# Weights through two raw slots of 1 MB instead of four of 512 KB

## The chip, the cores and the metric

The kernel runs on one core of one Trainium2 chip. The metric is the device time of one execution in microseconds, here the median of several runs. The engines are TensorE (PE: matmuls, and weight loads into the array as PEld), VectorE (DVE), ScalarE (ACT), GpSimd (POOL) and SyncE (SP), which here does nothing but issue transfers. Each engine works through its own list in order, and waits on semaphores for the others.

## The reference

Four transformer layers follow one another on a sequence of 256 tokens with 1024 channels, all in f32. Each is a mixer and a hidden layer, with an RMS norm ahead of each:

```python
def first_block(x, ...):
    h = h + stick_breaking_attention(hn, w_sb_in[i], w_sb_out[i])      # layer 0, 16 heads
    h = h + squared_relu_mlp(rms_norm(h, g_mlp[0]), w_mlp_up[0], w_mlp_down[0])
    h = h + retention(hn, w_ret_in[i], w_ret_out[i])                    # layer 1, 4 heads
    h = h + squared_relu_mlp(rms_norm(h, g_mlp[1]), w_mlp_up[1], w_mlp_down[1])
    return rms_norm(h, g_final)
def second_block(x, ...):
    x = x + gla_mixer(hn, ...)                                          # gated linear attention
    x = x + conv_ffn(hn, ffn_w_up[0], ffn_conv_w[0], ffn_conv_b[0], ffn_w_down[0])
    x = x + nsa_mixer(hn, nsa_w_in[b], nsa_w_o[b], *nsa_shared_kv(x, ...))
    x = x + conv_ffn(hn, ffn_w_up[1], ...)
    return rmsnorm(x, norm_final)
```

All weight matrices together are 212 MB; each number of them is used once.

## The kernel before, in words

The host lays the weight matrices out as 212 pieces `ws[g]` of 128 partitions by 2048 f32 (`PIECE`), 1 MB each, in the order in which PE uses them. Pieces 0 to 15 belong to the stick-breaking attention (`G_SB`), then come MLP 0 (16 to 47), retention (48 to 79), MLP 1 (80 to 111), gated linear attention (GLA, 112 to 127), the first convolutional hidden layer (FFN, 128 to 160), the sparse attention (NSA, 161 to 178) and the second FFN (179 to 211).

A piece passes four engines:

- SP brings it to the raw ring `ring`, which has `RAW` = 4 slots of half a piece (`HALF` = 1024 columns, 512 KB). Half q = 2g or 2g+1 of piece g goes to slot q % 4. The function is `stream`; from the fifth half on it waits until DVE has read the slot's last content (`lo_ready`). Landing is told on `weights_in[q % 4]`.
- ACT rounds the half to fp32r, `w_hi` (`hi_half`, line 1228; the split below).
- DVE writes what the rounding left out, `w_lo` (`lo_half`, line 1701; the remainder below).
- PE multiplies in three matmuls of fp32r (`mm3`, lines 565 to 567): high by high, high by low and low by high. It waits per half piece on `lo_ready` (`split`) and tells on `done` that it has finished a piece.

`w_hi` and `w_lo` have `RING` = 4 slots of a whole piece. ACT's and DVE's function `refill(g)` waits (ACT on `done`) until PE has finished piece g, and then splits piece g + 4 into its slot, both halves in a row. The calls of `refill` stand in ACT's and DVE's lists at places that are written out by hand between their other work (norms, evacuations, softmax parts). Both engines work in order: whatever stands behind a split that waits for its transfer waits too.

At the start SP issues the four quarter pieces of x (`x_half`) between the first halves. In the stick-breaking attention ACT's list has the splits of pieces 5, 6 and 7, then the first pair's two sigmoids (`sb_sigmoids(0)`, lines 1364 and 1365), the splits of pieces 8 and 9, the second pair's sigmoids, and the copy of the first pair's transposed weights (`sb_copy(0)`, line 1369). PE's list has the transposes `sb_turn(0)` (line 772) ahead of piece 6, and the products `sb_av(0)` (line 783) in the middle of it; the first wait for the sigmoids (over DVE's scan, line 1918, and its product, line 1923, and POOL, line 420), the second for the copy. At the start of NSA, ACT's list has `refill(G_NSA + 2)`, `ns_raw_(0)` (lines 1534 and 1535), `refill(G_NSA + 3)`, `ns_raw_(1)`, the normed input (`tiles("7b", 0, ...)`), and so on, up to the gates (line 1611), which PE transposes.

Of the kernel before, what the change touches and what calls it, by code (L numbers as in the profile page):

```python
# [28 lines left out]
HALF = PIECE // 2  # L29
RAW = 4  # L30
# [43 lines left out]
G_END = 212  # L74
# [3 lines left out]
def build(nc, ws, small, narrow, tables, decay, rows, x_in, out):  # L78
    from contextlib import ExitStack
    ctx = ExitStack()  # L80
    with ctx:
        def sb(name, shape, dt=F32):
            return ctx.enter_context(nc.sbuf_tensor(name, shape, dt))

        def sem(name):
            return ctx.enter_context(nc.semaphore(name))

        ring = sb("ring", [P, RAW, HALF])
# [108 lines left out]
        x_loaded = [[sem(f"x_loaded{t}{c}") for c in range(2)] for t in range(TT)]  # L197
        quarter_done = sem("quarter_of_stage_done")
        tab_in, row_in = sem("tables_loaded"), sem("row_loaded")
        weights_in = [sem(f"weights_in{s}") for s in range(RAW)]  # L200
        hi_ready, lo_ready = sem("piece_hi"), sem("piece_lo")
        done = sem("piece_done")
        n_ready = sem("narrow_split")
# [20 lines left out]
        def plus(n, turn, each):  # L224

            return n if turn is None else turn * each + n
# [136 lines left out]
        @block.sync  # L363
        def _(sp):
            def x_half(t, c):
                v = slice(c * 512, (c + 1) * 512)
                sp.dma_start(h[:, t, v], x_in[t * P:(t + 1) * P, v]).then_inc(x_loaded[t][c], 16)

            def stream(q, turn=None):

                if turn is not None or q >= RAW:
                    sp.wait_ge(lo_ready, plus(q - RAW + 1, turn, RAW))
                g, c = q // 2, (q % 2) * HALF
                src = ws[g][:, c:c + HALF] if turn is None else \
                    ws[bass.ds(turn * (RAW // 2) + g, 1), :, c:c + HALF].rearrange("a p n -> p (a n)")
                sp.dma_start(ring[:, q % RAW, :], src).then_inc(weights_in[q % RAW], 16)

            x_half(0, 0)
            stream(0)
            stream(1)  # L380
            x_half(1, 0)
            x_half(0, 1)
            stream(2)
            x_half(1, 1)
            stream(3)
            turns = (2 * G_END - RAW) // RAW
            with sp.Fori(0, turns) as turn:
                for q in range(RAW, 2 * RAW):
                    stream(q, turn)
            for q in range(RAW + turns * RAW, 2 * G_END):  # L390
                stream(q)
            for t in range(TT):
                for c in range(2):
                    v = slice(c * 512, (c + 1) * 512)
                    sp.wait_ge(xs_ready[c], t + 1)
                    sp.dma_start(out[t * P:(t + 1) * P, v], xs[:, t, v]).then_inc(stored, 16)
            sp.wait_ge(stored, 32 * TT)
# [812 lines left out]
        def _(act):  # L1210
# [13 lines left out]

            def hi_half(q):
                c = (q % 2) * HALF
                act.wait_ge(weights_in[q % RAW], 16 * (q // RAW + 1))
                A(w_hi[:, q // 2 % RING, c:c + HALF], ring[:, q % RAW, :], ACT.Copy).then_inc(hi_ready, 1)  # L1228

            def hi(g):  # L1230
                hi_half(2 * g)
                hi_half(2 * g + 1)
# [101 lines left out]
            act.wait_ge(gains_ready, 1)  # L1334
            tiles(0, 0, part=(0, 1))
            hi_half(0)
            hi_half(1)
            tiles(0, 1, part=(0, 1))
# [345 lines left out]
        def _(dve):  # L1684
# [551 lines left out]
            def ns_cmp_p(c):  # L2236

                s, _, l = ns_cmp(c)
                dve.wait_ge(nsa_cmp_exp, c + 1)
                sees = tab[:, C_CMUL:C_CMUL + TT * CMP].rearrange("p (t n) -> p t n", n=CMP)[:, :, 0:1]  # L2240
                link(V.tensor_reduce(l, s, AX.X, ALU.add))
                link(V.reciprocal(l, l))
                link(V.tensor_tensor(l, l, ns_gate[:, :, 8 * c:8 * c + 8], ALU.mult))
                link(V.tensor_tensor(l, l, sees.broadcast_to([P, TT, 8]), ALU.mult))
                V.tensor_tensor(s, s, l.unsqueeze(3).broadcast_to([P, TT, 8, CMP]), ALU.mult).then_inc(nsa_cmp_p, 1)
# [327 lines left out]
```

## Time and profile before

| | |
|---|---|
| median of 3 runs | 1360.02 us (1358.62 to 1360.3) |
| the profiled execution's own time | 1360.86 us |
| its span, first to last instruction | 1359.1 us |
| PE busy | 1337.8 us, 98% |
| DVE, ACT, POOL busy | 907.8, 726.0, 121.3 us |
| `ring<-ws` transfers | 424 of 512 KB, median 4.8 us from issue to landing |
| read from HBM over the span | 169 GB/s |

The busy time of an engine is the union of its instructions. The profile's times start at the first instruction. "Landing" is the time from the issue of a transfer by SP to its last semaphore update. Idle time stands with what ended it.

### The profile page before, as it was taken

To read this page: it belongs to the slowest core of one execution; us is meant where nothing else is said; L and a number is where in the kernel's file an instruction comes from. 1 tells how busy PE (TensorE), PEld (TensorE's weight loads), DVE (VectorE), ACT (ScalarE), POOL (GpSimd) and SP (SyncE) were. 2 spreads that over 40 slices of the span, in tenths; PEclk is the share of its full clock that TensorE was granted. 3 is DMA by queue.
4 is the path that set the end of the run, shared out by engine and by line. 5 is a ranking of instruction groups with operands and counts; after the bars stand their busy time and mean duration, and the time that the engine had idled before them with its cause. 6 is when DMAs were issued, how large, how long until landed. Compare 5 with 4: busy or idle time off the path is not lost.

```text
span 1359.1 us, 23120 instructions
## 1 busy us (share of the span) xinstructions
PE 1337.8 (98%) x8826; PEld 1198.2 (88%) x8826; DVE 907.8 (67%) x1417; ACT 726.0 (53%) x1155; POOL 121.3 (9%) x123
## 2 busy tenths in 40 slices
PE   9999999999999999999999999999999999999998
PEld 8888989889987889999888889999988877999996
DVE  5757655557645647555567569777868775787776
ACT  6655544445334536444464457555557656665553
POOL 0002000002500000000001300000002233000000
PEclk9999999999999999999999999999999999999999
DMA  7535655555553456555554345555554411365551
GB/s 255 187 125 205 219 185 187 187 185 183 189 186 124 156 171 217 185 187 187 187 169 146 105 156 196 195 184 190 170 188 162 166 53 51 126 210 187 184 184 72
DMA packets 63887, 231.09 MB, mean 170 GB/s; under 512 B 7088, under 2 KB 7344, under 8 KB 63792
## 3 DMA queue, kind: packets, MB, share of 16 engines
q1 hardware_dynamic: 62208, 224.42, 49.2%
q10 hardware_dynamic: 1584, 5.31, 1.1%
q8 instruction: 70, 1.15, 0.3%
q14 instruction: 25, 0.20, 0.0%
HBM read 228.66 MB, written 1.05 MB: 169 GB/s over the span
## 4 chain that ended last, share of the span: by engine, by line
PE 89%; DVE 5%; ACT 2%; issue 2%; DMA 1%; POOL 1%; POOLq 0%; DVEq 0%; SPq 0%; ACTq 0%
PE ps L565 27%; PE ps L567 27%; PE ps L566 27%; DVE w_lo L1701 2%; PE ps L934 1%; DVE x_lo L1721 1%; ACT w_hi L1228 1%; PE ps L537 1%; PE ps L1094 1%; PE ps L1125 1%; DMA ring<-ws 1%; PE ps L1107 1%; ACT x_hi L1248 1%; PE ps L858 1%; PE ps L783 0%
## 5 line engine op out<-in xcount | busy, mean ns | idle before, releaser
L1701 DVE TENSOR_TENSOR w_lo<-ring,w_hi 128x1024 fp32r<-128x1024 f32 x424 | 514.8, 1253 | 174.2 <-ACT w_hi L1228 173.8
L1228 ACT ACTIVATE w_hi<-ring 128x1024 fp32r<-128x1024 f32 x424 | 429.5, 1052 | 232.8 <-PE ps L567 181.3
L565 PE MATMUL ps<-x_hi,w_hi 128*128 128x256 f32 x1600 | 455.0, 284 | 0.5 <-DVE x_lo L1721 0.5
L566 PE MATMUL ps<-x_lo,w_hi 128*128 128x256 f32 x1600 | 452.7, 283 | 0.0
L567 PE MATMUL ps<-x_hi,w_lo 128*128 128x256 f32 x1600 | 452.7, 283 | 0.0
L565 PEld LDWEIGHTS ps<-x_hi,w_hi 128*128 128x128 f32 x1600 | 306.8, 192 | 4.1 <-issue 3.0
L566 PEld LDWEIGHTS ps<-x_lo,w_hi 128*128 128x128 f32 x1600 | 306.9, 192 | 1.1
L567 PEld LDWEIGHTS ps<-x_hi,w_lo 128*128 128x128 f32 x1600 | 306.8, 192 | 0.0
L565 PE MATMUL ps<-w_hi,y_hi 128*128 128x512 f32 x560 | 220.3, 393 | 0.4 <-DVE y_lo L1753 0.4
L566 PE MATMUL ps<-w_lo,y_hi 128*128 128x512 f32 x560 | 218.3, 390 | 0.0
L567 PE MATMUL ps<-w_hi,y_lo 128*128 128x512 f32 x560 | 218.1, 389 | 0.0
L567 PEld LDWEIGHTS ps<-w_hi,y_lo 128*128 128x128 f32 x560 | 105.1, 188 | 22.3
L565 PEld LDWEIGHTS ps<-w_hi,y_hi 128*128 128x128 f32 x560 | 105.3, 188 | 21.9 <-issue 0.8
L565 PE MATMUL ps<-w_hi,x_hi 128*128 128x512 f32 (+1 forms) x304 | 122.7, 404 | 0.8 <-DVE w_lo L1701 0.8
L566 PEld LDWEIGHTS ps<-w_lo,y_hi 128*128 128x128 f32 x560 | 105.3, 188 | 20.1
L567 PE MATMUL ps<-w_hi,x_lo 128*128 128x512 f32 (+1 forms) x304 | 116.3, 383 | 0.0
L566 PE MATMUL ps<-w_lo,x_hi 128*128 128x512 f32 (+1 forms) x304 | 115.8, 381 | 0.0
L411 POOL TENSOR_TENSOR stat<-stat,power 128x1 f32<-128x1 f32 x20 | 11.7, 588 | 876.6 <-DVE stat L1696 695.5
L1748 DVE SCALAR_TENSOR_TENSOR arena<-ps,arena 128x512 f32<-128x512 f32 x64 | 44.0, 688 | 65.7 <-PE ps L567 63.9
L1314 ACT ACTIVATE arena<-arena,sm 128x256 f32<-128x256 f32 x88 | 48.2, 595 | 52.0 <-DVE arena L1748 52.0
L565 PEld LDWEIGHTS ps<-w_hi,x_hi 128*128 128x128 f32 x304 | 58.0, 191 | 15.9 <-issue 5.4
L1248 ACT ACTIVATE x_hi<-ps,sm 128x128 fp32r<-128x128 f32 x128 | 35.7, 377 | 63.9 <-PE ps L537 63.9
(219 smaller groups left out, 1260.8 us busy)
## 6 DMA issues: line engine op xcount, KB each, us to landing
ring<-ws SPq DMA_DIRECT2D x424, 512.0 KB, 4.8
tab<-tables ACTq DMA_DIRECT2D x3, 550.0 KB, 5.3
rowg<-rows ACTq DMA_DIRECT2D x3, 512.0 KB, 6.2
h<-x SPq DMA_DIRECT2D x4, 256.0 KB, 6.1
out<-arena SPq DMA_DIRECT2D x4, 256.0 KB, 2.2
arena<-decay ACTq DMA_DIRECT2D x1, 768.0 KB, 8.6
sm<-small ACTq DMA_DIRECT2D x1, 642.0 KB, 4.7
arena<-narrow ACTq DMA_DIRECT2D x1, 296.0 KB, 2.9
```

Source lines behind the costliest of these rows:

```text
L537: r = nc.tensor.transpose(ps[:, base + k // 2, t * T + (k % 2) * P:t * T + (k % 2 + 1) * P], h[:, t, k * P:(k + 1) * P], ident)
L565: mm(o, lh, rh, start=start, stop=False, skip_group_check=True)
L566: mm(o, lh, rl, start=False, stop=False, skip_group_check=True)
L567: return mm(o, ll, rh, start=False, stop=stop, skip_group_check=True)
L858: r = mm(ps[:, rt_o[hd][t], :], rt_s[:, hd, t * P:(t + 1) * P], rt_v[:, 0, hd * 512:(hd + 1) * 512], start=True, stop=t == 0)
L934: r = mm(o, keys, q, start=True, stop=True, skip_group_check=True)
L1094: r = mm(ps[:, 4 + i, P * t:P * (2 * t + 1)], ns_qr[v, pr, t * P:(t + 1) * P], ns_kd[v, br, pr // 2, 0:P * (t + 1)], start=t == 0, stop=Tr ...
L1228: A(w_hi[:, q // 2 % RING, c:c + HALF], ring[:, q % RAW, :], ACT.Copy).then_inc(hi_ready, 1)
L1248: r = A(dst[:, k, t * P:(t + 1) * P], ps[:, base + b, t * T + (k % 2) * P:t * T + (k % 2 + 1) * P], ACT.Copy, scale=gain(n, k))
L1314: r = A(conv[:, u % 2, e, :], conv_in[:, u % 2, e, :], ACT.Identity, scale=par(u, 4 + e), bias=par(u, 6 + e))
L1701: V.tensor_tensor(w_lo[:, g % RING, v], ring[:, q % RAW, :], w_hi[:, g % RING, v].bitcast(F32), ALU.subtract).then_inc(lo_ready, 1)
L1748: return V.scalar_tensor_tensor(dst, src.rearrange("p (a t) -> p a t", t=T), by, sc.unsqueeze(1).broadcast_to([P, 2, T]), ALU.mult, ALU.mult)
```

## The change

SP brings a piece in one transfer of 1 MB to a raw slot of a whole piece, of which there are two: slot g % 2 is the halves 2(g % 2) and 2(g % 2) + 1 of the same `ring`. The slot is free when both remainders of piece g - 2 are written. There are two landing semaphores instead of four, and both halves of a piece wait on the same one. At the start SP issues x's first quarter, piece 0, x's other three quarters, piece 1. What ACT, DVE and PE do, and their order, stays; each half is still split by itself.

```diff
-        weights_in = [sem(f"weights_in{s}") for s in range(RAW)]
+        weights_in = [sem(f"weights_in{s}") for s in range(RAW // 2)]
...
-            def stream(q, turn=None):
-
-                if turn is not None or q >= RAW:
-                    sp.wait_ge(lo_ready, plus(q - RAW + 1, turn, RAW))
-                g, c = q // 2, (q % 2) * HALF
-                src = ws[g][:, c:c + HALF] if turn is None else \
-                    ws[bass.ds(turn * (RAW // 2) + g, 1), :, c:c + HALF].rearrange("a p n -> p (a n)")
-                sp.dma_start(ring[:, q % RAW, :], src).then_inc(weights_in[q % RAW], 16)
+            def stream(g, turn=None):
+
+                if turn is not None or g >= 2:
+                    sp.wait_ge(lo_ready, plus(2 * g - 2, turn, RAW))
+                src = ws[g] if turn is None else ws[bass.ds(turn * 2 + g, 1), :, :].rearrange("a p n -> p (a n)")
+                dst = ring[:, 2 * (g % 2):2 * (g % 2) + 2, :].rearrange("p a n -> p (a n)")
+                sp.dma_start(dst, src).then_inc(weights_in[g % 2], 16)
 
             x_half(0, 0)
             stream(0)
-            stream(1)
             x_half(1, 0)
             x_half(0, 1)
-            stream(2)
             x_half(1, 1)
-            stream(3)
-            turns = (2 * G_END - RAW) // RAW
+            stream(1)
+            turns = (G_END - 2) // 2
             with sp.Fori(0, turns) as turn:
-                for q in range(RAW, 2 * RAW):
-                    stream(q, turn)
-            for q in range(RAW + turns * RAW, 2 * G_END):
-                stream(q)
+                for g in range(2, 4):
+                    stream(g, turn)
+            for g in range(2 + turns * 2, G_END):
+                stream(g)
...
-                act.wait_ge(weights_in[q % RAW], 16 * (q // RAW + 1))
+                act.wait_ge(weights_in[q // 2 % 2], 16 * (q // RAW + 1))
```

SP's list at the start of the program, with - for before and + for the change (`ring<-ws` is a piece or a half piece of the weights, `h<-x` a quarter of x):

```order
 L367 DMA h<-x 128x512
-L376 DMA ring<-ws 128x1024 x2
-L367 DMA h<-x 128x512 x2
-L376 DMA ring<-ws 128x1024
-L367 DMA h<-x 128x512
-L376 DMA ring<-ws 128x1024
...
+L375 DMA ring<-ws 128x2048
+L367 DMA h<-x 128x512 x3
+L375 DMA ring<-ws 128x2048
```

The four half-piece issues in front of the loop have become two issues of a whole piece, and the last three quarters of x now all stand between them.

ACT's list in the stick-breaking attention before, from the splits of piece 5 to the first split of piece 9 (`piece_done` is PE's `done`):

```order
L1228 ACTIVATE w_hi<-ring 128x1024 [waits weights_in2,piece_done]
L1228 ACTIVATE w_hi<-ring 128x1024 [waits weights_in3]
L1228 ACTIVATE w_hi<-ring 128x1024 [waits weights_in0,piece_done]
L1228 ACTIVATE w_hi<-ring 128x1024 [waits weights_in1]
L1228 ACTIVATE w_hi<-ring 128x1024 [waits weights_in2,piece_done]
L1228 ACTIVATE w_hi<-ring 128x1024 [waits weights_in3]
L1364 ACT_TABLE_LOAD
L1364 ACTIVATE arena<-ps 128x768 [waits sb_z]
L1365 ACTIVATE arena<-ps 128x768
L1228 ACTIVATE w_hi<-ring 128x1024 [waits weights_in0,piece_done]
L1228 ACTIVATE w_hi<-ring 128x1024 [waits weights_in1]
L1228 ACTIVATE w_hi<-ring 128x1024 [waits weights_in2,piece_done]
```

The same place of ACT's list in the change:

```order
L1225 ACTIVATE w_hi<-ring 128x1024 [waits weights_in1,piece_done]
L1225 ACTIVATE w_hi<-ring 128x1024 [waits weights_in1]
L1225 ACTIVATE w_hi<-ring 128x1024 [waits weights_in0,piece_done]
L1225 ACTIVATE w_hi<-ring 128x1024 [waits weights_in0]
L1225 ACTIVATE w_hi<-ring 128x1024 [waits weights_in1,piece_done]
L1225 ACTIVATE w_hi<-ring 128x1024 [waits weights_in1]
L1361 ACT_TABLE_LOAD
L1361 ACTIVATE arena<-ps 128x768 [waits sb_z]
L1362 ACTIVATE arena<-ps 128x768
L1225 ACTIVATE w_hi<-ring 128x1024 [waits weights_in0,piece_done]
L1225 ACTIVATE w_hi<-ring 128x1024 [waits weights_in0]
L1225 ACTIVATE w_hi<-ring 128x1024 [waits weights_in1,piece_done]
```

Nothing has moved; the first split of a piece now waits for the semaphore that its second half also waits for. Line numbers behind SP's part are three lower in the change.

## Rows read from the trace of the kernel before

**Rows 1.** The page: span, and busy us, share, instructions of each engine.

```profile
span 1359.1 us, 23120 instructions
...
PE 1337.8 (98%) x8826; PEld 1198.2 (88%) x8826; DVE 907.8 (67%) x1417; ACT 726.0 (53%) x1155; POOL 121.3 (9%) x123
```

**Rows 2.** PE's waits: waiting line, its releaser, us in total, times, longest.

```profile
PE ps L1160 <- ACT arena L1611: 2.3, 1, 2.3
PE ps L1107 <- POOL arena L507: 1.5, 1, 1.5
...
PE ps L537 <- DVE h L1775: 0.9, 1, 0.9
```

**Rows 3.** ACT's waits, whole span: its waits for a weight transfer.

```profile
ACT w_hi L1228 <- DMA ring<-ws: 50.7, 59, 3.6
```

**Rows 4.** Line 376 between 1118 and 1127 us: two halves, issued 7.4 us apart.

```profile
DMA to landing us min/median/max: 3.5/3.6/3.7
```

**Rows 5.** Line 376 between 237.5 and 239.5 us: two halves, with nothing else under way.

```profile
L376 SPq DMA_DIRECT2D ring<-ws x2: 332/332/333, 237.8 to 238.9; - x2
...
DMA to landing us min/median/max: 3.8/4.3/4.8
```

**Rows 6.** Line 376 between 1 and 2 us: the first two halves.

```profile
L376 SPq DMA_DIRECT2D ring<-ws x2: 424/424/425, 1.3 to 1.7; - x2
...
DMA to landing us min/median/max: 4.9/5.4/5.8
```

**Rows 7.** ACT's timeline, first 55 us: start, us, instruction, [idle before].

```profile
6.43 2.16 ACT L1228 ACTIVATE w_hi<-ring 128x1024 fp32r<-128x1024 f32 x2
...
31.33 2.00 ACT L1228 ACTIVATE w_hi<-ring 128x1024 fp32r<-128x1024 f32 x2
...
48.57 0.79 ACT L1364 ACTIVATE arena<-ps 128x768 f32<-128x768 f32 x1
...
49.95 0.81 ACT L1369 ACTIVATE arena<-ps 128x768 f32<-128x768 f32 x1
```

**Rows 8.** The chain of waits, 26 to 58 us: start, us, what.

```profile
34.94 5.75 DMA ring<-ws
40.71 1.06 ACT w_hi L1228
...
51.43 0.81 PE ps L783 x12
```

**Rows 9.** PE's timeline at 47.7 us.

```profile
47.69 0.87 PE L772 MATMUL ps<-sm,arena 128*128 128x128 f32 x6 [0.39 <-POOL arena L420]
```

**Rows 10.** SP's timeline at 19.3 us.

```profile
19.26 0.33 SPq L376 DMA_DIRECT2D ring<-ws  x1
```

**Rows 11.** The chain of waits, 984 to 994 us.

```profile
984.82 5.94 DMA ring<-ws
```

**Rows 12.** SP's timeline at 1006.7 us.

```profile
1006.74 0.33 SPq L376 DMA_DIRECT2D ring<-ws  x1
```

**Rows 13.** ACT's timeline at 1019.5 us.

```profile
1019.52 1.06 ACT L1228 ACTIVATE w_hi<-ring 128x1024 fp32r<-128x1024 f32 x1 [1.10 <-DMA ring<-ws]
```

**Rows 14.** DVE's timeline at 1037.2 us.

```profile
1037.24 3.32 DVE L1701 TENSOR_TENSOR w_lo<-ring,w_hi 128x1024 fp32r<-128x1024 f32 x2 [0.28 <-ACT w_hi L1228]
```

**Rows 15.** SP's timeline at 1064.4 us.

```profile
1064.44 0.33 SPq L376 DMA_DIRECT2D ring<-ws  x1
```

**Rows 16.** ACT's timeline, 1064 to 1080 us.

```profile
1068.64 2.08 ACT L1228 ACTIVATE w_hi<-ring 128x1024 fp32r<-128x1024 f32 x2
...
1073.20 0.43 ACT L1546 ACTIVATE arena<-ps 128x120 f32<-128x120 f32 x2 [0.22 <-PE ps L1039]
```

**Rows 17.** Two stretches: PE, PEld, DVE, ACT, POOL busy, granted clock, DMA share, GB/s.

```profile
1050.20:1052.20 2.00, 0.00 (x0) 0.00 (x0) 2.00 (x4) 1.48 (x3) 0.00 (x0) 1.00 0.20 68
1052.20:1059.00 6.80, 6.00 (x28) 5.22 (x29) 4.85 (x14) 5.40 (x13) 0.00 (x0) 0.50 0.82 270
```

**Rows 18.** ACT's timeline at 1275.1 us, in the second FFN.

```profile
1275.13 1.09 ACT L1314 ACTIVATE arena<-arena,sm 128x256 f32<-128x256 f32 x2 [2.28 <-DVE arena L1748]
```

## The prediction

> **What bounds the kernel now.** I read the page first: TensorE (PE) works in 1337.8 of 1359.1 us [rows 1]. So nothing on another engine costs time unless it makes PE wait, and every wait that it does make PE take is added to the end, since PE runs its list in order. The view of PE's waits shows few: the longest, 2.3 us, is for ScalarE (ACT) at line 1611 in the last attention [rows 2]. The weights' own row says where the change can bite: ACT stood 59 times, 50.7 us in all, waiting for a half piece to land [rows 3]. Nearly all of that is hidden now, because the four split slots `w_hi`/`w_lo` let PE run behind. It is not hidden where ACT's list holds something that PE needs soon behind a weight split.
>
> **What one transfer costs, L.** A half piece alone lands 3.5 to 3.7 us after its issue [rows 4]. Two halves issued 1.1 us apart land after 3.8 and 4.8 us [rows 5]: 5.9 us from the first issue for the whole megabyte. The trace has no 1 MB transfer. Lower bound: at the start, where the queue is full, halves issued at 1.3 and 1.7 us land after 4.9 and 5.8 us, at 6.2 and 7.5, so the second 512 KB takes 1.3 us more [rows 6]; 3.6 + 1.3 = 4.9 us. Upper bound: the pair's 5.9 us, as the same bytes pass the same engines. I take L = 5.3, an estimate between the two, because the second half of a pair starts 1.1 us late, when the engines are still at work on the first. The Trainium skill ("DMA: Bandwidth & Descriptors", "Anatomy of one DMA") gives 2.0 us plus the bytes by 436 GB/s, which makes 4.4 us; it fits transfers from another queue, and by it the sum below would be about 2 us. The half alone took 0.4 us more than that formula's 3.2 us here.
>
> **What the change does to a slot.** Before, a half slot is refilled once its own half is split; now both halves must be split, so a piece's transfer starts when only its second half used to start. The second half then lands about when it did (4.8 against L), the first about 1.1 + 5.3 - 3.8 = 2.6 us later, and the second split, which ran at the landing of its half, now runs 0.95 us behind the first (below). The 424 half issues become 212; SP only waits, so this saves nothing on the path. From the first split of a piece to the issue that its slot frees: the first split of piece 5 begins at 31.33 and the half that its slot lets through is issued at 34.94, 3.61 us [rows 7, 8]; two splits in a row take 2.00 us, each 1.06, so the second begins 0.95 behind the first. One slot thus turns round in L + 3.61 = 8.9 us for every second piece, where PE takes one piece each 6.4 us (1359.1 by 212 pieces): supply is enough, only its lateness counts.
>
> **Start.** The first piece lands at 7.5 instead of 6.2; the queue is full, so at the same time as its second half did. Its first split ran at 6.43 [rows 7], so PE starts 1.07 us late.
>
> **Term A, the first attention.** ACT has the splits of pieces 5, 6 and 7 in front of the first two sigmoids, and of 8 and 9 in front of the next two. Already now the chain passes through the second half of piece 7: issue 34.94, landing after 5.75, split 40.71, and then sigmoid, scan, product, and the transposes at 47.69, before which PE stood 0.39 us [rows 8, 9]. The odd pieces share a slot. The second half of piece 3 was issued at 19.26 [rows 10]; with the start's 1.07, piece 3 is now issued at 20.33, lands at 20.33 + L, and each next odd piece L + 3.61 later. Piece 7 lands at 27.55 + 3L = 43.5; its second split starts at 44.4 instead of 40.71, 3.7 us late, and PE stands about 3.0 us in front of the transposes (3.7 + 0.39 - 1.07). Piece 9 lands at 31.16 + 4L = 52.4; its two splits take 1.9 us to the start of the next operation [rows 7], so the second sigmoids start at 54.3 instead of 48.57, 5.7 us late. The copy after them (49.95, 0.81 us long) is what PE needs at 51.43: 0.67 us of cover [rows 7, 8]. **A = 4L - 16.2 = 5.0 us**, which contains the start and the first stall. The even pieces share the other slot and land between the odd ones, ahead of ACT. From piece 10 on ACT waits for PE to free a split slot before it splits, and the transfer is there by then.
>
> **Term B, the end of the first FFN.** The chain runs through the second half of piece 162, issued at 984.82, 5.94 us to landing, split at 990.79; PE then waits 0.9 us for the residual [rows 2, 11]. Now both halves come at 984.82 + L and the second split 0.95 later: **B = L - 5.02 = 0.3 us**.
>
> **Term C, the start of the last attention.** Piece 165 is issued at 1006.74 [rows 12], its slot is refilled 3.61 after it lands, so piece 167 lands at 1010.35 + 2L and its second split starts at 1011.30 + 2L = 1021.9 instead of 1019.52 [rows 13]. Behind it ACT has no pause until it has split the normed input, and VectorE (DVE) then runs without a pause but for 0.28 us at 1037.24 [rows 14] up to the gates for which PE stands 2.3 us: **C = 2L - 8.22 - 0.28 = 2.1 us**.
>
> **Term D, a little later.** Piece 175 is issued at 1064.44 [rows 15]; its second split starts at 1065.39 + L = 1070.7. Before, the two took 2.08 us from 1068.64, that is to say the second started at 1069.66. ACT is 1.0 us late and has 0.22 us of pause before the copy at 1073.20 [rows 16], from which the chain goes over DVE and GpSimd to PE's 1.5 us wait [rows 2]: **D = L - 4.5 = 0.8 us**.
>
> **Clock.** Before, PE had nothing to do from 1050.2 to 1052.2, and then its granted clock was 0.50 for 6.8 us, the 1.2 GHz level [rows 17]. The stall of 3.0 us that A makes near 48 us is longer. If it is answered in the same way, 6.8 us at half clock lose 3.4 us of matmuls, of which 5.0 - 3.7 = 1.3 us fall into time in which PE would stand anyway: between 0 and 2.1 us, and I take 1.2. The fall that exists at 1052 stays as it is.
>
> **What I cost at nothing.** In both FFNs one split in three arrives at a half that has just landed; its second split is now about 1.1 us later. It is hidden by ACT's own pause behind it (next work at 1275.13 after 2.28 us idle, waiting for DVE [rows 18]). If that pause were gone, each of some 14 such places would cost up to 1.1 us. The MLPs, retention and GLA splits run 5 us or more ahead of PE and wait for PE at the loop's pace; their first pieces come 1 to 2.5 us later and eat cover alone.
>
> **Sum.** 5.0 + 0.3 + 2.1 + 0.8 + 1.2 = 9.4 us. The profiled execution took 1360.86, so 1370.3; it lies 0.84 above the median of the three runs shown (1360.02), so **1369.4 us** as a median. With L = 4.9 and no fall of the clock: 3.4 + 0 + 1.3 + 0.4 = 5.1, so 1365. With L = 5.9: 7.4 + 0.9 + 3.3 + 1.4 + 2.1 = 15.1, so 1375.
>
> **Rivals.** (1) A megabyte lands fast. Its rows are 8 KB instead of 4 KB and half as many descriptors are written; at L = 4.4, half a microsecond under my lower bound, the terms are 1.4 + 0 + 0.3 + 0 = 1.7 us: 1361.7, no difference that shows. For it: the 1.3 us for 512 KB in a full queue [rows 6]. Against it: no pair in the trace comes near it. The Trainium skill's rule on that page ("Rules for kernel authors": at least 1 MiB per DMA for bandwidth) points this way; its page "Perfetto Trace Analysis", "DMA Optimizations", points the other way (smaller pieces may start sooner where the DMA engines are mostly idle); with this trace's chain waiting on the landing of a half at 40.7 us, the second agrees with it, and no run yet shows the first. (2) Faster: both chains of A and B run through halves that took 5.75 and 5.94 us because another half was in flight. One transfer per piece ends these collisions. But for a gain over 2.7 us the stalls behind them must vanish (0.4 + 0.9 + about 1.3 of the 2.3 us), and that needs L at 3.6, the time of half the bytes: about 1357. (3) The lateness adds up in the FFNs, where ACT is never far ahead: 14 times 0.6 us, 8 us on top, 1377. Against it: DVE there waits for PE in each chunk, so nothing accumulates. (4) ACT's order is more elastic than I think, and only the start's 1.07 and C remain: 3.2 us, 1363.
>
> **How the numbers follow.** Forecast with its mechanism (A to D, L from 4.9 to 5.9): 0.68. Rival 1: 0.14. Rival 2: 0.04. Rival 3: 0.07. Rival 4: 0.07. 0.2% of 1360 is 2.7 us, about what a measurement of this kernel can tell from nothing. Slower by more: 0.68 + 0.07 + most of rival 4, 0.80. Within: rival 1 and a part of rival 4, 0.16. Faster: 0.04. The range goes from 1362.5, where rival 4 begins, to 1375.5, where L = 5.9 ends; below it stand most of rivals 1 and 2 (0.15), above it 0.05 or so.
>
> **What the profile will show.** The median landing of `ring<-ws` at 5.3 us (over 5.9 or under 4.6 makes me wrong in size). PE's waits: a new one of about 3 us at the first attention's transposes (line 769 there, three up from 772), another of about 1.4 us at the products after them, the wait for the gates at 4.4 instead of 2.3, and the one on GpSimd at 2.3 instead of 1.5. ACT's waits for `ring<-ws` fewer, as the second half never waits, and longer. PE's granted clock at a half for some microseconds near 50. The time of the FFNs unchanged: the span from piece 140 to 158 to 0.2 us. I am wrong if PE's waits in the first 60 us stay under 2 us, or if the loss stands in the FFNs.

## The result, and the profile after

The changed kernel takes 1366.37 us, the median of five runs (1365.28 to 1368.22), against 1360.02 us before: 6.35 us more. The ratio to the runs of before is 1.005, its 95% interval 1.0038 to 1.0062, so it is slower by more than the 0.2% that a measurement can tell. The forecast was 1369.4 in a range from 1362.5 to 1375.5. The profiled execution took 1368.22, the slowest of the five, 7.36 us over the profiled one of before; a second profile of the same kernel (below) ended 4.54 us after before's, so what repeats has to be kept apart from what one execution shows. The lines of the changed part and behind stand three lower than before (L375 for L376, L1225 for L1228, L780 for L783).

The page and the queue of the weights, first that of after:

```profile
span 1366.5 us, 22278 instructions
...
PE 1339.5 (98%) x8826; PEld 1198.7 (88%) x8826; DVE 907.2 (66%) x1417; ACT 724.5 (53%) x1155; POOL 122.8 (9%) x123
...
q1 hardware_dynamic: 31680, 224.41, 45.6%
```

Against [rows 1], PE's busy time grew by 1.7 us of the 7.4; the rest is time in which it stood. The transfers' own engines are busy for less, not for more: 45.6% of the span against 49.2% for the same queue (`q1`) before.

What one transfer costs (the view of the tile `ring`), and ACT's waits for it (releaser, us in total, times, longest):

```profile
DMA to landing us min/median/max: 4.6/4.8/8.1
```

```profile
ACT w_hi L1225 <- PE ps L564: 167.8, 57, 7.5
ACT w_hi L1225 <- DMA ring<-ws: 110.5, 67, 4.5
```

The megabyte lands in 4.8 us, where I had taken 5.3. ACT's waits for it went from 50.7 us in 59 waits [rows 3] to 110.5 us in 67: longer, as I said, but not fewer. Sixty more us of waiting on ACT cost 6 us at the end: PE's waits, which follow, show that nearly all of them stand in front of a split that PE does not need yet.

PE's waits of after (waiting line, releaser, us in total, times, longest), to be read against [rows 2]:

```profile
PE ps L780 <- ACT arena L1366: 2.9, 3, 1.1
PE ps L1157 <- ACT arena L1608: 2.3, 1, 2.3
PE ps L769 <- POOL arena L417: 1.6, 1, 1.6
PE ps L1104 <- POOL arena L504: 1.6, 1, 1.6
PE ps L562 <- DVE y_lo L1718: 1.3, 1, 1.3
...
PE ps L534 <- DVE h L1772: 1.0, 1, 1.0
```

The transposes' wait at L769 grew from 0.39 [rows 9] to 1.6. The products at L780 waited once, 0.8 us near 85 us, before; that wait is unchanged and two of about 1 us are new. For `y_lo` PE waited once, 0.4 us, before; it now waits three times, the longest 1.27 us. The waits for the gates and for GpSimd, on which two of my terms ran, stand as they were. Where the waits lie is told by PE's timeline:

```profile
49.42 0.44 PE L769 MATMUL ps<-sm,arena 128*128 128x128 f32 x2 [1.61 <-POOL arena L417]
...
54.13 0.33 PE L780 MATMUL ps<-arena 128*64 128x128 f32 x2 [0.97 <-ACT arena L1366]
...
117.09 0.44 PE L780 MATMUL ps<-arena 128*64 128x128 f32 x4 [1.10 <-ACT arena L1366]
...
1036.78 1.99 PE L534 MATMUL ps<-sm,h 128*128 128x128 f32 x8 [0.40 <-DVE y_lo L1718]
...
1042.90 0.35 PE L562 MATMUL ps<-y_hi,w_hi 128*128 128x256 f32 x1 [1.27 <-DVE y_lo L1718]
```

The same two instructions of the first attention began at 47.69 and 51.43 before [rows 8, 9]: 1.73 and 2.70 us later now.

ACT's timeline shows what is late (each pair of splits is one piece; 5, 6, 7, 8 and 9 in this order):

```profile
33.11 2.01 ACT L1225 ACTIVATE w_hi<-ring 128x1024 fp32r<-128x1024 f32 x2 [1.20 <-DMA ring<-ws]
36.58 2.01 ACT L1225 ACTIVATE w_hi<-ring 128x1024 fp32r<-128x1024 f32 x2 [1.47 <-DMA ring<-ws]
41.50 2.01 ACT L1225 ACTIVATE w_hi<-ring 128x1024 fp32r<-128x1024 f32 x2 [2.90 <-DMA ring<-ws]
...
46.22 2.00 ACT L1225 ACTIVATE w_hi<-ring 128x1024 fp32r<-128x1024 f32 x2
49.97 2.01 ACT L1225 ACTIVATE w_hi<-ring 128x1024 fp32r<-128x1024 f32 x2 [1.75 <-DMA ring<-ws]
51.89 0.79 ACT L1361 ACTIVATE arena<-ps 128x768 f32<-128x768 f32 x1
...
53.27 0.81 ACT L1366 ACTIVATE arena<-ps 128x768 f32<-128x768 f32 x1
```

Pieces 5, 7 and 9 share a slot. Their first splits begin at 33.11, 41.50 and 49.97, a step of 8.4 us, which is 4.7 to 4.8 of landing and 3.65 to 3.72 from the landing to the next issue. The second sigmoids follow at 51.89 instead of 48.57, and the copy that PE needs at 53.27 instead of 49.95: 3.32 us late, of which 0.67 were covered [rows 7, 8], so 2.65, close to the 2.70 of PE's row.

A table of the lateness gives the whole sum: the time at which PE signals the end of a piece, less the same in the trace of before. The second line is the second profile of the same kernel (run e8_after_again).

| us later than before, at the end of piece | 0 (at 15 us) | 6 (55) | 14 (118) | 158 (986) | 160 (1000) | 165 (1030) | 167 (1044) | 169 (1060) | 176 (1151) | span |
|---|---|---|---|---|---|---|---|---|---|---|
| after | 0.48 | 2.77 | 3.94 | 3.94 | 4.02 | 4.01 | 7.01 | 7.13 | 7.39 | 7.4 |
| after, again | 0.20 | 2.56 | 4.54 | 4.49 | 4.41 | 4.40 | 5.20 | 4.20 | 4.56 | 4.6 |

The second line has 2.0 us between pieces 6 and 14, 1.2 of it at piece 14 as in the first; the other 0.8 goes with a wait of 0.7 us at the products at 63 us, behind piece 10, which landed in 7.4 us there and in 4.8 in the first profile.

From piece 14 to piece 158, 870 us with the MLPs, the retention, the GLA and a whole FFN, nothing is lost, and nothing behind piece 176. The same stretch, shifted by the 3.94 us (PE, PEld, DVE, ACT, POOL busy, granted clock, DMA share, GB/s), first before, then after:

```profile
130.00:980.00 850.00, 847.54 (x5334) 764.08 (x5333) 544.06 (x725) 429.31 (x596) 61.76 (x53) 1.00 0.53 178
```

```profile
133.94:983.94 850.00, 847.53 (x5334) 764.08 (x5333) 544.60 (x725) 429.10 (x596) 59.05 (x53) 1.00 0.50 178
```

### The profile page after: what moved, and what is told of

Its sections match the earlier page's. It is cut to its first block, busy times and chain, and to the rows that moved or that the text cites. A ratio compares the mean times of both kernels' runs of the same rounds, so it can differ in the third digit from the quotient of the medians.

```text
span 1366.5 us, 22278 instructions
## 1 busy us (share of the span) xinstructions
PE 1339.5 (98%) x8826; PEld 1198.7 (88%) x8826; DVE 907.2 (66%) x1417; ACT 724.5 (53%) x1155; POOL 122.8 (9%) x123
## 3 DMA queue, kind: packets, MB, share of 16 engines
q1 hardware_dynamic: 31680, 224.41, 45.6%
## 4 chain that ended last, share of the span: by engine, by line
PE 83%; DVE 7%; ACT 4%; DMA 4%; issue 2%; POOL 0%; SPq 0%; POOLq 0%; DVEq 0%; ACTq 0%
PE ps L562 25%; PE ps L564 25%; PE ps L563 25%; DMA ring<-ws 4%; DVE w_lo L1698 3%; ACT w_hi L1225 2%; PE ps L931 1%; DVE x_lo L1718 1%; PE ps L1122 1%; PE ps L1091 1%; PE ps L534 1%; ACT x_hi L1245 1%; PE ps L855 1%; PE ps L780 0%; DVE arena L2254 0%
## 5 line engine op out<-in xcount | busy, mean ns | idle before, releaser
L1225 ACT ACTIVATE w_hi<-ring 128x1024 fp32r<-128x1024 f32 x424 | 425.4, 1052 | 278.6 <-PE ps L564 167.8
L562 PEld LDWEIGHTS ps<-w_hi,x_hi 128*128 128x128 f32 x304 | 58.1, 191 | 16.2 <-issue 5.4
L564 PEld LDWEIGHTS ps<-w_hi,x_lo 128*128 128x128 f32 x304 | 58.0, 191 | 11.3
```

Source lines behind the costliest of these rows:

```text
L562: mm(o, lh, rh, start=start, stop=False, skip_group_check=True)
L564: return mm(o, ll, rh, start=False, stop=stop, skip_group_check=True)
```

## The experiments

Each was timed beside the kernel before, whose median was 1360.2 us with each of them. Unless it says otherwise, a time is the median of five runs.

### One half of the change at a time

The change has two effects on a piece: its transfer is issued only when both halves of the slot are free, and its first split runs only when all of it is there. The kernel before can have each with its 512 KB transfers. First the late issue alone:

```diff
-                    sp.wait_ge(lo_ready, plus(q - RAW + 1, turn, RAW))
+                    sp.wait_ge(lo_ready, plus(q - RAW + 2 - q % 2, turn, RAW))
```

> The kernel before with one part of the change: the first half of a piece is issued only when both remainders of the piece two before are written, right ahead of the second half; two transfers, four semaphores, each half still split as soon as it has landed. Theory M (what costs is when the halves can be split: a late issue and a landing that is told for both at once, read by ACT in order): here the first half lands some 3.7 us after the issue, the second about 4.9, so the second split is where it was before; 0 to 1.5 us slower than before. Theory S (a transfer of 1 MB is itself slower or collides more): no large transfer here, 0. Theory I (the late issue is the whole cause): 6 us slower, as the changed kernel.

1361.44 us (1359.52 to 1364.19, 11 runs), ratio 1.0015 (1.0007 to 1.0024): about 1 us. Its lateness is 0.35 us at piece 6 and 0.91 at piece 14. That is within what theory M gave, and it refutes theory I. The profiled execution, the fastest of the eleven, even ended 1.3 us before that of before, mostly because its clock never fell near 1050 (2.5 us less, told below). Then the whole landing alone:

```diff
                 act.wait_ge(weights_in[q % RAW], 16 * (q // RAW + 1))
+                if q % 2 == 0:
+                    act.wait_ge(weights_in[q % RAW + 1], 16 * (q // RAW + 1))
```

> The kernel before with the other part: halves are issued as before, but ACT waits for both halves before it splits the first. M: the second split of a piece that is waited for comes 0.95 us later than before, and in the first attention that adds up over pieces 3, 5, 7 and 9: 2 to 4 us slower, with a new wait of PE at the copy (line 1369) of about 1 us. S: 0. I: 0.

1367.99 us (1366.64 to 1370.0), ratio 1.006 (1.0047 to 1.0073). Its waits on PE are those of the changed kernel:

```profile
PE ps L783 <- ACT arena L1371: 3.2, 3, 1.3
...
PE ps L772 <- POOL arena L420: 1.5, 1, 1.5
...
PE ps L565 <- DVE y_lo L1723: 1.3, 1, 1.3
```

So most of the loss is this: ACT may not start on a first half that has landed. The expectation had the kind right and the size wrong: 2 to 4 us were forecast and 7.8 measured. In the profile the lateness at the end of the first attention is 4.3 us, 0.7 of it there since piece 0, which is near the forecast; the last attention (1.7 us more at piece 167), the residual at piece 160 (0.4) and the rest were not in it. Both together, still in two transfers, are the changed kernel but for the size of a transfer (and the place of x's quarters among the first issues, which stays as before):

> Both parts together, and still two transfers of 512 KB per piece: all of the change but the size of the transfer. M: as the changed kernel, 5 to 7 us slower than before, PE's waits in the first attention like those of the changed kernel (1.6 and 1.0 us, and 1.1 at 117 us). S: 0, as before. I: 6.

1374.18 us (1369.84 to 1378.66, 6 runs), ratio 1.0101 (1.0084 to 1.0118). That is 14.0 us, more than the two parts add up to (1.2 and 7.8), about twice the 5 to 7 us that theory M gave, and 7.8 us more than the changed kernel (7.2 more than the one with 4 KB rows below, which was timed together with it). The two transfers of a piece, issued one behind the other, are both there after a median of 5.27 us, where one megabyte takes 4.80. On the chain of the first attention it is more: pieces 3, 5, 7 and 9 were there after 6.54, 5.79, 5.25 and 5.18 us, the megabytes of the changed kernel after 4.90, 4.73, 4.67 and 4.77. The lateness at piece 6 is 7.34 us instead of 2.77, which is 4.6 of the 6.2 us between the two profiles. PE's view of waits has

```profile
PE ps L1107 <- POOL arena L507: 3.0, 1, 3.0
PE ps L783 <- ACT arena L1371: 2.5, 2, 1.7
...
PE ps L772 <- POOL arena L420: 2.2, 1, 2.2
PE ps L763 <- DVE arena L1750: 2.1, 1, 2.1
```

The large transfer by itself is thus a gain of 7 to 8 us over two small ones under the same waits. The change loses because in this ring it comes only together with the waits.

### Is it the size or the length of a row?

A megabyte transfer has rows of 8 KB, a half had 4 KB. Here the weights lie in memory as two halves one behind the other, so that one transfer brings the megabyte in 4 KB rows:

```diff
-                src = ws[g] if turn is None else ...
-                dst = ring[:, 2 * (g % 2):2 * (g % 2) + 2, :].rearrange("p a n -> p (a n)")
+                src = ws[g].rearrange("c p n -> p c n") if turn is None else ...
+                dst = ring[:, 2 * (g % 2):2 * (g % 2) + 2, :]
```

> The changed kernel with the weights laid out in HBM as two blocks of 512 KB per piece, so that one transfer of 1 MB is made of 4 KB rows instead of 8 KB ones. If the 8 KB rows are what made the megabyte land in 4.8 us instead of the 5.3 that was forecast, the median landing goes to 5.2 to 5.9 and the time rises by 3 us or more over the changed kernel (the sum's slope is about 8 us for each us of landing). If the row's length does not matter, landing 4.8 and the time of the changed kernel within 1.5 us.

1367.0 us (1365.84 to 1367.31), ratio 1.005 (1.0037 to 1.0063), with a landing of

```profile
DMA to landing us min/median/max: 4.7/4.9/8.1
```

The length of a row changes the landing by 0.07 us and the time by nothing that can be told. What makes 4.8 of 5.3 is not the rows; one transfer in place of two is what is left.

### The order on ACT

If the lateness costs only where ACT has something urgent behind a split, it should vanish when the urgent thing is put ahead. In the first attention (on the changed kernel, and in the same way on the kernel before) the first sigmoids move ahead of the splits of piece 7, the second sigmoids and the first copy ahead of those of piece 9, and the copy for pair 6 ahead of those of piece 17; DVE's first weighting moves ahead of its remainders of piece 7:

```diff
-            for g in range(1, 4):
-                refill(G_SB + g)
+            refill(G_SB + 1)
+            refill(G_SB + 2)
...
             sb_sigmoids(0)
+            refill(G_SB + 3)
             refill(G_SB + 4)
-            refill(G_SB + 5)
...
                 sb_copy(p)
+                if p == 0:
+                    refill(G_SB + 5)
...
             refill(G_SB + 12)
+            sb_copy(6)
             refill(G_SB + 13)
```

> The changed kernel with another order on ACT and DVE in the first attention alone: the first sigmoids stand ahead of the split of piece 7, the second sigmoids and the first copy ahead of that of piece 9, the copy of pair 6 ahead of that of piece 17; DVE's scan of the first pair ahead of piece 7's remainders. Theory M (PE's new waits there come from ACT's sigmoids and copies that stand behind splits which wait for a landing): the waits of 1.6, 1.0 and 1.1 us go, 3 to 4 us faster than the changed kernel, some 2 to 3 us over the kernel before, what is left being the start (0.5) and the last attention (1 to 3). Rival (PE waits there for its weights, or the late pieces hold it up in another way): the time stays within 1 us of the changed kernel, the waits move to line 562 on w_lo.

> The same new order in the kernel before. M: it can win only what PE waits there now, 0.4 us at the first transposes: 0 to 0.5 us faster than before, not to be told from nothing. If it wins 2 us or more, the order was the cause of loss in both kernels.

The changed kernel so ordered: 1362.76 us (1360.95 to 1364.16, 11 runs), ratio 1.0018 (1.0009 to 1.0027), 3.6 to 4.0 us under the changed kernel. The kernel before so ordered: 1359.32 (1357.77 to 1360.18, 11 runs), ratio 0.9993 (0.9984 to 1.0003), not to be told from before. Under the same new order the two kernels are 3.4 us apart, where they were 6.35. ACT's timeline of the first (pieces 6, 7, 8 and 9):

```profile
36.40 2.00 ACT L1225 ACTIVATE w_hi<-ring 128x1024 fp32r<-128x1024 f32 x2 [1.13 <-DMA ring<-ws]
38.42 1.28 ACT L1361 ACT_TABLE_LOAD   x1
...
41.81 2.01 ACT L1225 ACTIVATE w_hi<-ring 128x1024 fp32r<-128x1024 f32 x2 [0.57 <-DMA ring<-ws]
44.86 2.00 ACT L1225 ACTIVATE w_hi<-ring 128x1024 fp32r<-128x1024 f32 x2 [1.04 <-DMA ring<-ws]
48.06 0.81 ACT L1361 ACTIVATE arena<-ps 128x768 f32<-128x768 f32 x1 [1.19 <-PE ps L762]
...
49.46 0.82 ACT L1366 ACTIVATE arena<-ps 128x768 f32<-128x768 f32 x1
```

The table load and the sigmoids now fill the time in which ACT stood for piece 7; the splits of piece 7 still begin at 41.81, no earlier than in the changed kernel (41.50). The lateness at piece 6 is 0.26 us (0.71 from the start, less 0.45 that the order gains), and at piece 14 still 0.26. The transfer is as late as in the changed kernel, and PE's three new waits are gone. That shows the mechanism of the first attention, theory M, and refutes the rival, by which the waits would have moved to the weights.

### The first piece in two transfers

```diff
+            sp.dma_start(ring[:, 0, :], ws[0][:, 0:HALF]).then_inc(first_in, 16)
+            sp.dma_start(ring[:, 1, :], ws[0][:, HALF:PIECE]).then_inc(weights_in[0], 16)
```

> The changed kernel, but piece 0 comes in two transfers with a semaphore each, so that its first split can start as before. M: PE's first matmul on weights starts 0.4 to 0.5 us earlier, at 8.8; all of the odd pieces behind it come 0.4 earlier too, so 0.3 to 0.8 us faster than the changed kernel. Rival (the start is of no matter, since the first attention's chain is set by landings): 0.

1365.39 us (1364.09 to 1368.56), ratio 1.0039 (1.0025 to 1.0053); its interval overlaps the changed kernel's, so a gain of 0.3 to 0.8 us can neither be shown nor ruled out by the times. In the profile, which is that of the slowest of the five, the lateness at piece 0 is still 0.53 us. The rows of PE and ACT say why, first this run, then the changed kernel:

```profile
1.07 4.56 PE L721 MATMUL ps<-ones 128*128 128x128 f32 x20 [1.07 <-POOL ones L403]
5.95 1.14 ACT L1250 ACTIVATE x_hi<-ps,sm 128x128 fp32r<-128x128 f32 x4 [3.21 <-PE ps L536]
6.97 2.02 ACT L1230 ACTIVATE w_hi<-ring 128x1024 fp32r<-128x1024 f32 x2
```

```profile
1.07 4.25 PE L719 MATMUL ps<-ones 128*128 128x128 f32 x20 [1.07 <-POOL ones L401]
5.64 1.14 ACT L1245 ACTIVATE x_hi<-ps,sm 128x128 fp32r<-128x128 f32 x4 [2.90 <-PE ps L534]
6.89 2.00 ACT L1225 ACTIVATE w_hi<-ring 128x1024 fp32r<-128x1024 f32 x2
```

In this run the first half landed at 6.1, 4.8 us after its issue, and waited for ACT, which had the first tiles of the input before it. In the changed kernel the piece landed at 6.9, 5.6 us after its issue, just as ACT came free; the weights cost ACT about 0.2 us there (an estimate from these rows; 0.1 in the second profile). The landing of the input is not what differs: its first quarter was there at 4.24 us in this run and at 4.35 in the other. PE's twenty matmuls on `ones` differ, which wait for no transfer and stand in PE's list ahead of the transposes of the input: 4.56 us against 4.25. In the twelve profiles they took 3.88 to 4.64 us, and the end of piece 0 goes with them. The four kernels whose issues and first split are those of before have it at -0.07 us (late issue), 0 (before), 0.35 and 0.81 us (before with one and with both reorderings) against before. So the changed kernel's 0.48 and 0.20 us lie within what one execution differs from another, and do not show the start's term. The run with the whole landing does: its twenty matmuls took 4.06 us, its split began at 7.14, when the second half had landed, and it was 0.70 us late at piece 0.

### The changed kernel once more, and the last attention

> The changed kernel unchanged, for a second profile. Piece 167 landed 7.2 us after its issue in the first profile, and PE lost 3.0 us at the start of the last attention there. If that landing was a chance of that execution, it is 4.7 to 5.2 here and the loss there about 1 us; the losses in the first attention (2.3 and 1.2 us) repeat to 0.3 us. If it is a property of the place, 7 us and 3 us again.

1366.75 us (1365.4 to 1368.38), ratio 1.0055 (1.0041 to 1.0069). The waits of the first attention are there again (L769 1.6 us, L780 four times up to 1.1 us, one of them behind the slow piece 10 as told above; so the second loss was 2.0 us and not 1.2), but piece 167, issued at 1019.57, landed in 5.0 us and not in 7.2 as in the first profile. The lateness that pieces 166 and 167 add was then 0.80 us and not 3.0. In the first profile the chain of waits ran through this one landing:

```profile
1010.74 4.74 DMA ring<-ws
...
1019.20 7.23 DMA ring<-ws
```

Of the six profiles with megabyte transfers that were taken in all, four have this landing at 6.8 to 7.4 us (and 2.6 to 3.0 us of lateness here, in the three of them that keep this order), and two at 5.0 (0.8 and 0.9 us).

Could the order help here too? On the changed kernel with the first reordering, and on the kernel before with it, the two groups of four copies (`ns_raw_`) move ahead of the splits of pieces 167 and 168:

```diff
-            refill(G_NSA + 2)
             ns_raw_(0)
-            refill(G_NSA + 3)
+            refill(G_NSA + 2)
             ns_raw_(1)
+            refill(G_NSA + 3)
```

> The changed kernel with the first attention's order as in the reordering run (1362.8 us), and in the last attention ScalarE's two groups of four copies (line 1531 of the changed kernel) each ahead of the splits of pieces 167 and 168, which they stood behind. Theory M (the lateness of a piece costs only where ScalarE's list holds something that TensorE needs soon behind its splits): the 2.5 us of copies fall into the 4.5 us that ScalarE stands idle for piece 167, TensorE's waits of 0.4 and 1.3 us at 1036 and 1043 shrink where they exist, and the kernel gains 0.5 to 1.5 us: 1361.3 to 1362.3, and it comes within 0.2% of the kernel before. Rival F (the landing itself and the two splits of ScalarE and VectorE behind it set the time there, whatever is put ahead of them): 1362.8, unchanged.

> The kernel before with both reorderings. Theory M: 1359.3 as with the first attention's alone, less 0 to 0.5 us in the last attention, where the kernel before has no wait at 1036 to 1043: 1358.8 to 1359.3, and the distance to the changed kernel with both reorderings is 2 to 3 us, that of the start and of the rest. Rival F: 1359.3.

Neither expectation held. 1365.56 us (1364.95 to 1367.38), ratio 1.0041 (1.0027 to 1.0055), and 1364.18 us (1363.08 to 1366.12, 9 runs), ratio 1.0028 (1.0018 to 1.0038): the order costs 2.8 and 4.9 us. ACT's rows of the first:

```profile
1022.42 2.01 ACT L1225 ACTIVATE w_hi<-ring 128x1024 fp32r<-128x1024 f32 x2 [0.30 <-DMA ring<-ws]
1027.47 0.63 ACT L1534 ACTIVATE arena<-arena 64x512 f32<-64x512 f32 x1 [3.04 <-DVE arena L1748]
...
1030.05 2.01 ACT L1225 ACTIVATE w_hi<-ring 128x1024 fp32r<-128x1024 f32 x2
```

The second group of copies waits for a DVE instruction that stands behind DVE's remainders of piece 167, and these wait for ACT's splits of it. So the splits of piece 168 begin at 1030.05, where the first reordering alone had them at 1026.75; DVE's remainders follow (1031.14), then `y_lo` (1034.57), and PE stands at the transposes:

```profile
PE ps L534 <- DVE y_lo L1721: 3.1, 1, 3.1
```

In both kernels PE's granted clock then fell to 0.50, the 1.2 GHz level, for 3.4 us (from 1035.5 in the first, after the wait of 3.1 us, and from 1037.0 in the second, after one of 2.3), where neither kernel with the first reordering alone has a fall there. Wait and fall together are most of the 5.1 and 4.9 us of lateness that the profiles gain between the ends of pieces 165 and 166.

A copy moved ahead of a split is only a gain if what it waits for does not itself stand behind that split on another engine. I moved it without reading DVE's list.

## Why the prediction was right, and where it was not

**Direction and place.** Right. With half slots ACT begins on the first half; with whole ones it stands until all has landed, and PE pays where its next input is behind the split on ACT. The run with the whole landing alone (+7.8 us) and the reordering in the first attention (3.6 to 4.0 us back) show it. For the last attention it is read from the trace alone, since the reordering there failed. The rival that ACT's order is elastic is refuted: it had to be made so.

**L, the size that was off.** I took the middle, 5.3, between 4.9 and 5.9; it is 4.8, just under the lower bound, which came from two halves issued 0.5 us apart in a full queue [rows 6]. Two transfers in a row cost 5.27 in the run with both parts, so the bound was a bound on two transfers, and one is cheaper by about 0.5. The Trainium skill's formula for another queue ("DMA: Bandwidth & Descriptors", "Anatomy of one DMA") gave 4.4 us as an estimate; the trace, with 4.8, stands between it and my value. With 4.8 in place of 5.3 my sum is 3.0 + 0 + 1.1 + 0.3 and no fall of the clock, 4.4 us.

**Start.** Forecast 1.07, measured 0.48 and 0.20, of which waiting for the weights explains 0.1 to 0.2. The first megabyte landed 5.6 us after its issue at 1.26, at 6.9 and not 7.5. The rest is within the spread of PE's first matmuls, told with the run of the first piece.

**Term A.** Its form held: 4L - 16.2 at 4.8 is 3.0, measured 2.77 and 2.56 at piece 6. It holds the start at 1.07; with the measured one it would be 2.4 and 2.1, and the slot's turn makes up a part of the difference: 3.61 by [rows 7, 8], it was 3.65 to 3.72 from landing to issue, three times. The split between the two waits was wrong (1.6 and 1.0 instead of 3.0 and 1.4), as the start and L are less.

**The term that I missed.** At 117 us PE stands 1.10 us for the copy of pair 6, and the lateness grows by 1.17 (1.12 in the second profile's wait). I wrote that "from piece 10 on ACT waits for PE to free a split slot before it splits, and the transfer is there by then". For piece 17 it was not: before, its second half, issued at 106.69, landed after 4.1 us, and the second split began just then, at 110.84. Only the first half had time to spare, 0.9 us. ACT before (piece 17's splits, and the copy behind them):

```profile
109.87 2.04 ACT L1228 ACTIVATE w_hi<-ring 128x1024 fp32r<-128x1024 f32 x2 [2.26 <-PE ps L567]
111.81 0.80 ACT L1369 ACTIVATE arena<-ps 128x768 f32<-128x768 f32 x1
```

and after:

```profile
114.34 2.01 ACT L1225 ACTIVATE w_hi<-ring 128x1024 fp32r<-128x1024 f32 x2 [3.95 <-DMA ring<-ws]
116.25 0.79 ACT L1366 ACTIVATE arena<-ps 128x768 f32<-128x768 f32 x1
```

The two splits are one row, named as released by PE, and the landing that the second one waited for is not named. The copy is 4.44 us later, of which 2.77 is the kernel's lateness by then. With this term the sum at 4.8 is 5.6 us; the medians say 6.35.

**Term B.** 0.08 us later in the first profile, 0.08 earlier in the second (the residual's wait is 1.0 and 0.9, before 0.9); 0 by my term at 4.8.

**Term C.** The form 2L - 8.5 held (with 4.74 and 7.23 for the two landings it gives 3.5, measured 3.0; with 4.68 and 5.03, 1.2, measured 0.8). The place did not: PE pays at `y_lo`, ahead of the gates, and the gates' wait stays 2.3. What makes it 3.0 in one profile is the slow landing of piece 167. Over the five profiles with the original order here it is 2.0 us on average (3.0, 0.8, 0.9, 2.6, 2.6), 0.9 over my form at 4.8; with that the sum is 6.5 us against the 6.35 of the medians. That is an estimate, as nothing shows how often this piece is slow in the runs without a profile, nor why it is.

**Term D.** 0.8 forecast, 0.3 at 4.8; the lateness from piece 169 to 176 grows by 0.26 and 0.36.

**Clock.** 1.2 us forecast. The changed kernel's two profiles have no fall near 50 us. That it can come there is shown by the run with 4 KB rows, where PE stood 1.75 us at the same transposes and then had a granted clock of 0.50, the 1.2 GHz level:

```profile
49.98 0.85 PE L770 MATMUL ps<-sm,arena 128*128 128x128 f32 x5 [1.75 <-POOL arena L418]
```

```profile
50.50:53.90 3.40, 3.40 (x19) 3.40 (x18) 2.86 (x4) 3.35 (x5) 0.00 (x0) 0.50 0.24 29
```

It came in two of the four profiles with megabyte transfers and the first attention's old order, and the lateness at piece 6 was 3.8 and 3.5 us there, against 2.8 and 2.6 in the two without. Less what each already had at piece 0, that is 3.0 against 2.3 and 2.4, so the fall cost about 0.7 us. So the term was no mistake in kind; it is paid in some executions. PE had stood 1.75 and 1.8 us where the fall came and 1.6 where it did not; whether that decides it is not shown. In two of the same four, the fall near 1060 is shorter and gives 1.0 us back.

**At nothing.** FFNs, MLPs, retention and GLA: right to 0.1 us, and the rival in which lateness adds up there is refuted. The rival of the fast megabyte had part of the truth: L lay nearer to its 4.4 than I held likely, but the waits remained. The rival of the collisions is refuted in its result: under the same waits a single transfer is faster than two, by 7 to 8 us over the kernel, and those waits cost the kernel with two transfers 14.0.

**The total.** That 9.4 us lay as near to 6.35 as it did is in part luck. L and the clock made my sum 5.0 us too large (9.4 against 4.4), and the two terms that I did not have, the copy of pair 6 and the slow landing of piece 167, make 2.1 us the other way.

## What to carry to other kernels

A transfer in one piece is faster than two halves, but its consumer learns of it once, at its end; what counts is when the consumer may start, and what stands behind it on that engine. Before making transfers larger, list for each consumer which urgent instruction stands behind the one that waits for data, and for each wait that names another releaser, how long before it the data had landed: here one of 0.02 us stood behind a row that named PE. Putting the urgent instruction ahead of the split gave the changed kernel 3.6 to 4.0 us back and took the distance between the two kernels from 6.35 to 3.4 us; the same move made without reading the other engine's list cost more than it could bring.

## What the runs showed of the hardware

A megabyte on this queue lands in 4.8 us (median, 4.6 at least), two halves issued directly behind each other (0.5 us apart) in 5.27 from the first issue, and in 6.1 with the second 1.1 us behind the first (medians). Rows of 4 or 8 KB make 0.07 us of difference. Some landings take over 6 us, 7 to 15 of the 212 in each profile, and they are not spread at random: pieces 140 and 187 are among them in all six profiles with megabyte transfers (6.1 to 6.5 us), piece 43 in five, piece 167 in four; piece 1, issued behind x at the start, takes 8.0 to 8.7 us in all six. One of them on the chain costs more than most terms of my sum, and a median says nothing of it.

After the same wait of 2.3 us for the gates, PE's granted clock fell to 0.50, the 1.2 GHz level, for 6.8 us in the first profile of the changed kernel as before [rows 17]:

```profile
1059.50:1066.30 6.80, 6.29 (x30) 5.50 (x31) 4.70 (x15) 5.09 (x12) 0.05 (x1) 0.50 0.73 269
```

In its second profile the fall is half as long, which shows in the lateness as 1.0 us less at piece 169, and in the late-issue run it did not come at all, 2.5 us less:

```profile
1049.50:1056.30 6.80, 3.87 (x33) 3.23 (x32) 6.66 (x12) 5.76 (x7) 0.00 (x0) 1.00 0.46 149
```

Over the twelve profiles the fall behind this wait of 2.3 us lasted 6.8 us in five, 3.4 in five, and did not come in two. So equal waits are answered unequally, and up to 2.5 us between two single executions are no effect of an edit. Which of the three comes is not explained by anything that I read in the rows.
